# The first block's layer norms without barriers, and the inverse levels spread over four quarters of the array

## What is computed

```
x = layer_norm(x, ln0_g, ln0_b)
for l in range(DEPTH):                      # 2
    mix = hybrid_mixer(x, ...)              # pooling, differential attention, RWKV-7 in both directions
    x = layer_norm(alpha * x + mix, ln1_g[l], ln1_b[l])
    hid = square(relu(x @ w_up[l]))
    x = layer_norm(alpha * x + hid @ w_down[l], ln2_g[l], ln2_b[l])

def layer_norm(x, g, b):
    mu = mean(x); var = mean(square(x - mu))
    return (x - mu) * rsqrt(var + LN_EPS) * g + b
```

## Time and profile before

| | us |
|---|---|
| median of 3 runs | 4649.83 |
| lowest, highest | 4648.24, 4654.93 |
| the profiled execution | 4657.47 |
| its span, first to last instruction | 4655.7 |
| PE, DVE, ACT busy | 4436.1, 1408.8, 867.9 |
| mean granted TensorE clock | 0.968 |

### The profile page before, as it was taken

The page is one execution under the profiler, slowest core; times in us unless marked ns, Lnnn a source line. Parts: engine busy times, 40 slices in busy tenths (PEclk is TensorE's granted clock), DMA queues, the critical chain, the costliest instruction groups (busy, mean ns, idle before and its releaser), DMA issues.

```text
span 4655.7 us, 60696 instructions
## 1 busy us (share of the span) xinstructions
PE 4436.1 (95%) x25140; PEld 2927.2 (63%) x25140; DVE 1408.8 (30%) x3439; ACT 867.9 (19%) x2217; POOL 329.8 (7%) x274
## 2 busy tenths in 40 slices
PE   7899999989998999999998999899999999999999
PEld 3676674434443567775443444677887788788888
DVE  3665651020001556662111100331123331312232
ACT  3123320010000232221001000222222202222220
POOL 0122200000000022210000000000110000011000
PEclk8999999999999999999999999999999999999999
DMA  3001002212221110002221222111111121111111
GB/s 108 28 28 41 32 20 83 84 54 77 73 77 58 51 41 28 29 28 70 86 77 55 73 77 77 46 46 50 50 50 50 50 68 55 46 55 51 55 55 64
DMA packets 71343, 261.61 MB, mean 56 GB/s; under 512 B 7920, under 2 KB 7920, under 8 KB 70816
## 3 DMA queue, kind: packets, MB, share of 16 engines
q1 hardware_dynamic: 69168, 250.62, 15.7%
q10 hardware_dynamic: 1904, 7.11, 0.5%
HBM read 253.51 MB, written 4.19 MB: 55 GB/s over the span
## 4 chain that ended last, share of the span: by engine, by line
PE 91%; DVE 4%; ACT 3%; DVEq 1%; issue 1%; DMA 0%; ACTq 0%; SPq 0%
PE ps L2238 26%; PE ps L1420 25%; PE ps L2358 9%; PE ps L1589 4%; PE ps L2324 4%; PE ps L1439 2%; PE ps L1523 2%; PE ps L2268 2%; PE ps L824 2%; PE ps L831 1%; PE ps L790 1%; PE ps L2249 1%; PE ps L816 1%; PE ps L2259 1%; PE ps L1542 1%; PE ps L866 1%
## 5 line engine op out<-in xcount | busy, mean ns | idle before, releaser
L2238 PE MATMUL ps<-xT,ring 128*128 128x512 f32 x2656 | 1172.6, 600 | 58.0 <-ACTq L672 47.1
L2238 PEld LDWEIGHTS ps<-xT,ring 128*128 128x128 f32 x2656 | 507.3, 193 | 707.9 <-issue 707.9
L1420 PE MATMUL ps<-xT,ring 128*128 128x264 f32 (+2 forms) x3392 | 798.6, 391 | 17.3 <-DVE arena L1908 10.1
L1420 PEld LDWEIGHTS ps<-xT,ring 128*128 128x128 f32 (+1 forms) x3392 | 642.2, 193 | 137.4 <-DVE arena L1908 13.5
L2358 PE MATMUL ps<-arena,ring 128*128 128x512 f32 x1024 | 440.4, 592 | 2.4 <-ACT arena L2473 1.4
L2358 PEld LDWEIGHTS ps<-arena,ring 128*128 128x128 f32 x1024 | 194.2, 190 | 248.6 <-issue 248.6
L1420 PE MATMUL ps<-arena,ring 128*128 128x264 f32 (+1 forms) x1408 | 320.3, 385 | 2.3 <-DVEq L1809 2.3
L1420 PEld LDWEIGHTS ps<-arena,ring 128*128 128x128 f32 x1408 | 265.9, 191 | 46.4 <-issue 6.1
L1679 ACT ACTIVATE arena<-ps 128x264 f32<-128x264 f32 (+8 forms) x316 | 122.7, 389 | 710.4 <-PE ps L1420 618.2
L1053 ACT ACTIVATE arena<-ps 128x128 f32<-128x128 f32 (+1 forms) x268 | 103.2, 405 | 404.8 <-PE ps L2238 159.1
L2594 DVE TENSOR_TENSOR arena<-arena 128x512 f32<-128x512 f32 x64 | 44.3, 692 | 419.8 <-ACT arena L2473 419.8
(11 more groups left out here) (322 smaller groups left out, 5253.7 us busy)
## 6 DMA issues: line engine op xcount, KB each, us to landing
ring<-in_weights SPq DMA_DIRECT2D x467, 512.0 KB, 3.4
arena<-skew_dram ACTq DMA_DIRECT2D x8, 448.0 KB, 3.1
arena<-in_x SPq DMA_DIRECT2D x1, 2048.0 KB, 10.9
out_rows<-arena SPq DMA_DIRECT2D x8, 256.0 KB, 2.8
skew_dram<-arena ACTq DMA_DIRECT2D x4, 511.5 KB, 6.0
consts<-in_const SPq DMA_DIRECT2D x1, 1384.0 KB, 5.9
consts<-in_const ACTq DMA_DIRECT2D x1, 1252.0 KB, 5.5
arena<-in_buckets SPq DMA_DIRECT2D x1, 127.9 KB, 10.9
```

The lines of the kernel that those rows point to most:

```text
L1420: mm = pe.matmul(o[0:m, 0:cols.stop - cols.start], ws[:, k, 0:m], src[:, k, cols], start=k == 0, stop=k == nk - 1)
L2238: m = pe.matmul(o, w[:, k, :], src[:, k, 0:S], start=k == 0, stop=k == KD - 1)
```

## The change

Norms:
- The barriers go. PE waits for each tile of the normed `xT` by itself (`normed`), in the first projection behind a norm alone.
- Ahead of each norm but the first, DVE keeps a running sum `acc` of tiles 0 to 6 of `xT` as they are updated (`add_up`, one more tensor_tensor per tile from tile 1 to tile 6). The mean is then two matmuls: ones by `acc`, ones by tile 7. The first norm keeps 8.
- The mean isn't copied out: one scalar_tensor_tensor per tile subtracts it out of PSUM. The root reads the sum of squares from PSUM, with scale and bias. A one-element Sqrt ahead of the squares brings the table.
- Gain and bias: ACT does tiles 0 to 5, DVE tiles 6 and 7.
- In the first norm, the matmuls of the mean and of the squares come ahead of the bias lines on PE; ACT copies and stores the lines behind its part of the norm.

Inverse levels: for the second head the operands X, XT and W of block e lie in the other partition half, in the buffer of the other number where that is needed. `first_inverse`, `level_w` and `level_x` then use all four quarters in turn; `level_t` and both corners use the same ones as before. The number of instructions and their sizes stay.

```diff
-            def halves():
-
-                for n in range(NCH):
-                    for q in range(2):
-                        for h in range(2):
-                            e = q ^ h
-                            yield h, n, slice(HB * e, HB * e + HB), slice(HB * n, HB * n + HB)
+            half = [slice(HB * e, HB * e + HB) for e in range(2)]
+            quarters = [(n, h, e, slice(HB * n, HB * n + HB)) for n in range(NCH) for h in range(2) for e in (h, 1 - h)]
...
             def level_w(d, b, x):
...
-                for h, n, r, k in halves():
-                    m = pe.matmul(o[h][r, k], g1[d][h][r, n, 0, r], X[d][h][r, n, :], start=True, stop=True)
+                for n, h, e, k in quarters:
+                    r = half[e]
+                    m = pe.matmul(o[e][half[e ^ h], k], g1[d][h][r, n, 0, r], X[d][e ^ h][r, n, :], start=True, stop=True)
...
             def level_x(d, b):
...
-                for h, n, r, k in halves():
-                    m = pe.matmul(o[h][r, k], XT[d][h][r, n, :], W[d][h][r, n, :], start=True, stop=True)
+                for n, h, e, k in quarters:
+                    f = half[e ^ h]
+                    m = pe.matmul(o[e ^ h][half[e], k], XT[d][h][f, n, :], W[d][e][f, n, :], start=True, stop=True)
...
             def level_t(d, b):
...
-                for h, n, r, k in halves():
-                    m = pe.matmul(o[h][r, k], W[d][h][r, n, :], XT[d][h][r, n, :], start=True, stop=True)
+                for n in range(NCH):
+                    for e in range(2):
+                        for h in range(2):
+                            f = half[e ^ h]
+                            m = pe.matmul(o[h][f, HB * n:HB * n + HB], W[d][e][f, n, :], XT[d][h][f, n, :], start=True, stop=True)
...
+            def mean_of(it, bank):
+
+                pe.wait_ge(*at("ln_summed", it - 1))
+                pe.matmul(ps[:, bank, :], ones, acc, start=True, stop=False)
+                pe.wait_ge(*at("ln_ready", it, KD - 1))
+                pe.matmul(ps[:, bank, :], ones, xT[:, KD - 1, 0:S], start=False, stop=True).then_inc(STEPS["mean_made"][0], 1)
...
-                act.wait_ge(*at("ln_var", it))
-                act.activation(lnm[:, 1, :], lnm[:, 0, :], ACT.Sqrt).then_inc(STEPS["ln_root"][0], 1)
+                act.wait_ge(*at("var_made", it))
+                act.activation(lnm[:, 1, :], ps[:, banks[1], :], ACT.Sqrt, scale=1.0 / D, bias=lam[:, 8:9]).then_inc(STEPS["ln_root"][0], 1)
...
-                for j in range(KD):
+                for j in range(6):
                     act.wait_ge(*at("ln_scaled", it, j))
-                    act.activation(xT[:, j, 0:S], xT[:, j, 0:S], ACT.Identity, scale=g0[:, j:j + 1], bias=b0[:, j:j + 1])
-                act.drain()
+                    act.activation(xT[:, j, 0:S], xT[:, j, 0:S], ACT.Identity, scale=g0[:, j:j + 1], bias=b0[:, j:j + 1])\
+                       .then_inc(STEPS["ln_out_a"][0], 1)
```

More of the change, by code:

```diff
@@ L354, in build @@
         relu = rf.take(4, S)
+        acc = relu[:, 0, :]
         rl = Region()
@@ L2260, in turn, with mean_part, var_parts @@
                 tiles.close(m)
-            def layer_norm(base, it):
-                v = Maker(pe, lnV, base, v_made, v_taken)
-                for which, src, ready in (("mean", xT, "ln_ready"), ("var", sqr, "ln_sq")):
-                    o = v.open(which)
-                    for j in range(KD):
-                        pe.wait_ge(*at(ready, it, j))
-                        m = pe.matmul(o, ones, src[:, j, 0:S], start=j == 0, stop=j == KD - 1)
-                    v.close(m)
-                v.end()
+            def mean_part(it, bank, j):
+                pe.wait_ge(*at("ln_ready", it, j))
+                m = pe.matmul(ps[:, bank, :], ones, xT[:, j, 0:S], start=j == 0, stop=j == KD - 1, skip_group_check=True)
+                if j == KD - 1:
+                    m.then_inc(STEPS["mean_made"][0], 1)
+            def mean_of(it, bank):
[3 more added lines that the diff above has]
+                pe.matmul(ps[:, bank, :], ones, xT[:, KD - 1, 0:S], start=False, stop=True).then_inc(STEPS["mean_made"][0], 1)
+            def var_parts(it, bank):
+                for j in range(KD):
+                    pe.wait_ge(*at("ln_sq", it, j))
+                    m = pe.matmul(ps[:, bank, :], ones, sqr[:, j, :], start=j == 0, stop=j == KD - 1)
+                m.then_inc(STEPS["var_made"][0], 1)
             pe.wait_ge(c_loaded, 16)
@@ L2277, in _ @@
                 turn(a, f"x{j}", [xrow[:, t, j * P:(j + 1) * P] for t in range(4)])
+            for j in range(KD):
+                mean_part(0, BV[0], j)
+            var_parts(0, BV[1])
             pe.wait_ge(*at("relw", 0))
@@ L2383, in _, with layer_norm @@
                 act.drain().then_inc(STEPS["ln_ready"][0], 1)
-            for h in range(4):
-                for i in range(2):
-                    n = min(512, LINE - 512 * i)
-                    o = a.open(f"line{h}_{i}")
-                    a.close(act.activation(line[:, h, 512 * i:512 * i + n], o[:, 0:n], ACT.Copy))
-            a.end()
-            act.drain()
-            for h in range(4):
-                act.dma_start(skew_dram[h, :].rearrange("(p n) -> p n", n=LINE), line[:, h, 0:LINE])\
-                   .then_inc(skew_stored, 16)
-            act.wait_ge(skew_stored, 64)
-            def layer_norm(it, g0, b0, base, to_h=False):
+            def layer_norm(it, g0, b0, banks, to_h=False):
+                act.activation(lam[:, 9:10], ones[:, 0:1], ACT.Sqrt)
                 for j in range(KD):
@@ L2494, in _, with add_up @@
             dve.drain().then_inc(STEPS["relw"][0], 1)
-            def layer_norm(base, it):
-                v = Taker(dve, lnV, base, v_made, v_taken)
-                o = v.open("mean")
-                v.close(dve.tensor_scalar(lnm[:, 0, :], o, 1.0 / D, None, ALU.mult))
-                dve.drain()
+            dve.memset(lam[:, 8:9], LN_EPS)
+            dve.drain()
+            def add_up(j):
+                if 0 < j < KD - 1:
+                    dve.tensor_tensor(acc, xT[:, 0, 0:S] if j == 1 else acc, xT[:, j, 0:S], ALU.add)
+                    dve.drain()
+                if j == KD - 2:
+                    dve.sem_inc(STEPS["ln_summed"][0], 1)
@@ new lines, in layer_norm @@
+                for j in range(KD):
+                    dve.tensor_tensor(xT[:, j, 0:S], xT[:, j, 0:S], lnm[:, 0, :], ALU.mult).then_inc(STEPS["ln_scaled"][0], 1)
+                if to_h:
+                    return
+                dve.drain()
+                for j in range(6, KD):
+                    dve.tensor_scalar(xT[:, j, 0:S], xT[:, j, 0:S], g0[:, j:j + 1], b0[:, j:j + 1], ALU.mult, ALU.add)\
+                       .then_inc(STEPS["ln_out_v"][0], 1)
+                dve.drain()
+            l0 = K1_AT["ln0"][0]
```

136 lines of the change are left out of this document (61 added, 75 removed).

## The result

The changed kernel takes 4572.86 us (median; 4562.41 to 4580.16), the kernel before on the same chip 4652.38 (4648.24 to 4656.23). The ratio is 0.983, with a 95% interval from 0.981 to 0.985: 1.7% faster, 79.5 us. The forecast was 4574, and the time lies in its range.

What follows compares the result with a forecast made beforehand. PE, busy 95% of the span, was taken to bound the kernel, with 91% of the chain. Norms 50.5 plus levels 25 made 75.5 us: 4582 for a profiled execution, 4574 for the median; range 4560 to 4605.

Steps and rivals of the forecast that it cites:

- The norms: All five norms: shorter means, no copies of mean and variance, earlier projections; 50.5 us gained together.
- The running sum: Mean of a norm: two matmuls instead of eight, 5.34 us saved, with DVE's adds covered and costing nothing.
- The wait per tile: End of a norm: the projection needs only tile 0, starts 1.8 us after the scaling instead of 6.87, 5.1 earlier.
- The first norm: Bias lines moved behind the norm, made at half clock; first projection at 54.4 us, 5.4 gained (3.4 to 9.9).
- The norms behind the mixers: Layers 0 and 1: mean 5.34, copies 0.79 and 0.77, end 5.1; 12.0 us each, 24.0 for the two.
- The levels: Inverse levels and first inverses: four quarters at 14.6 ns a record; 3.1 us a group, 8 groups, 25 us gained.
- a quarter is a stream of its own: Inverse levels: each quarter takes about 58 ns a record, so four quarters in turn give 14.6 ns.
- rival 1: Inverse levels: four quarters go as two, 29.2 ns stays, the norms alone remain; 4599 us, chance 23%.
- rival 2: Inverse levels: a floor on record spacing leaves a third to half of the gain, 10 us; 4589 us, chance 16%.
- The five levels: Each group: a level takes 5.24 us instead of 5.74; four levels give 0.5 each, the fifth 0.2, 2.2 a group.
- The bounds that the prediction gave for the levels: Gain in the levels: 0 if four quarters go no faster, 60 us at 1.5 a level; 35 without the wait for W.
- Rival 3: Inverse levels: the clock falls, a level takes 8.0 us; 4691 us, chance 4%. Against: PE never stands longer than 0.7 us.

Runs made afterwards that it cites:

- eight_sums: The changed kernel with the mean of four norms made of eight matmuls again, no running sum and no adds on DVE: 4598.05 us, ratio 0.988.
- wait_all: The changed kernel, but the first projection behind a norm waits for all eight tiles before its first matmul: 4589.82 us, ratio 0.985.
- after_again: The changed kernel itself, the same program in another execution: 4571.74 us, ratio 0.982 of the kernel before.
- norms_only: The changed kernel with the old order of quarters in the inverse levels: 4607.15 us, ratio 0.989 of the kernel before.
- w_twice: The changed kernel with each matmul of level_w issued twice, 64 records more per level: 4627.95 us, ratio 0.994 of the kernel before.
- levels_only: The kernel before with the new inverse levels alone: 4633.6 us, ratio 0.9955.
- rows_apart: The changed kernel with the 16 matmuls of W, X and first inverse sorted, one row half's eight before the other's: 4584.54 us, ratio 0.984.

## Why the forecast came out

**The norms** (50.5, measured 54.0 by stages and 50.5 as a difference of medians). Each step is seen. The running sum is worth 4.8 to 5.2 us a norm, forecast 5.34 (`eight_sums`), and its adds are covered. The wait per tile gives 4.5 to 4.8 of the 5.1 forecast for the end of a norm (`wait_all`). The first norm came out at 5.4, since the lines did run at half clock, which was the choice there. The norms behind the mixers gave 1.1 and 1.5 more than 12.0: the sum of squares takes 7.15 us instead of 8.69. The stretch had a mean clock of 0.81 before, in the window's row of the kernel before:

```profile
1003.00:1011.90 8.90, 8.68 (x16) 3.60 (x16) 3.58 (x7) 5.52 (x9) 0.00 (x0) 0.81 0.01 2
```

I had kept the 8.69 as if it were work.

**The levels** (25, measured 18.7). That a quarter is a stream of its own was right, and with it that 32 records take 0.46 us; rival 1 and rival 2 fall by it. The two first inverses gave 0.91 us a group, forecast 0.94, thus 7.3 of the 18.7. The five levels gave 11.4 in all, forecast 17.6, and here a step failed: the one that counted matmuls by their spacing alone. At 15 ns a record PE asks for more instructions than come, and 11.3 us of stops that weren't in the sum are on the path. The prediction's argument that PE never stands longer than 0.7 us in a level fell with it: a stop of 1.17 us is shown above.

Without the stops the term would have been up to 30, so something else was mis-sized, in the other direction. It isn't the bare level: one with neither a stop nor other work of PE in it lasts 5.25 us (the fourth in layer 0's first group) or 5.45 (the third in layer 1's first), forecast 5.24. The trace puts 31 us down to DVE in the eight groups and not 60, but these can't be set side by side: the trace counts PE as busy until a matmul's end, 0.22 us behind its start, while the forecast counted waits from the spacing of starts. With the stops taken out, which is an estimate, since DVE catches up while PE stands, the first three levels gave 0.4 to 0.6 us each, forecast 0.5. The fourth gave about 1.0 in the six groups in which PE has other work in it; its waits for DVE are 0.05 to 0.22 us there. The fifth gave 0.6, forecast 0.2. The forecast priced the fourth as if it were bare and the fifth too low; why the fifth gave more isn't shown.

The bounds that the prediction gave for the levels don't follow from its own numbers: 5.74 less 3.74 is 2.0 us a level, 80 in all and not 60, and 25 with the wait for W of 0.7 a level taken out is 53 and not 35. The measured term lies below all of them.

**What was not in the sum**: 22.4 us of the profiled pair. 16.1 of it lies behind the last corner of each layer, where the kernel before runs at half clock for 17 us. The windows there, 9 to 26 us behind the corner of layer 0, of the kernel before and of the changed one:

```profile
648.00:665.00 17.00, 16.40 (x70) 14.59 (x72) 6.56 (x20) 3.95 (x12) 0.00 (x0) 0.50 0.00 0
```

```profile
625.00:642.00 17.00, 16.36 (x134) 14.57 (x134) 11.48 (x36) 6.94 (x21) 0.00 (x0) 1.00 0.01 2
```

134 records in the time of 70. It isn't a sure gain. In `after_again` the half clock stays away in layer 0 and is back for 17 us in layer 1:

```profile
2031.00:2050.00 19.00, 18.51 (x80) 15.40 (x81) 7.16 (x22) 4.17 (x13) 0.00 (x0) 0.55 0.00 1
```

In the traces of the kernel before and of `norms_only` it is there for 17 us in four layers of four. With the new levels, 20 layers of 10 traces (`w_twice` aside), it is missing in eight, shorter in ten (7 to 14 us) and full in two; `w_twice` has it for 17 and 14 us. What the new levels do to PE ahead of it, standing now and then and starting matmuls more densely, changes how the clock falls; by which rule, these runs don't settle. The clock as a whole also goes with the spread of the changed kernel: over four of its executions the span goes from 4560.6 to 4578.4 us as the mean clock goes from 0.975 to 0.972, and their product stays within 4 us. Over the whole trace the kernel before spends 296 us at half clock, the changed one 228 and `after_again` 252.

So that the forecast's time was met within 2 us is in part luck. Its terms were off in opposite ways: the levels gave 6.3 less, the norms 3.5 more, and the clock outside the edited stages gave some us that weren't in the sum, more in the profiled execution and fewer in the median one. How many of the median's 79.5 us are the clock's isn't shown; the two halves, run alone, sum to 74.5, and the difference lies within the intervals.

**Rival 3**, the clock falling inside the levels, didn't come in the changed kernel: the granted clock is 1.00 through the levels of all eight groups, and in the window from 155 to 184 us PE is busy 84%. In `levels_only` it falls 1.1 us before one corner, and in `w_twice` 4.7 us in the levels are at half clock.

## What to carry to other kernels

When matmuls are small, count instructions as well as their spacing: once they follow each other at 15 ns, the supply of instructions is a limit of its own, and it shows as "issue" idle time at equal distances in records, beside packets of 16 KB. In a norm across engines, the whole-tensor barriers are cheap to find and to remove: a wait per tile and a running sum kept beside the matmuls gave some 10 of the 13 us behind a mixer. And read the clock in the stretches behind the edit too, on more than one execution, before a gain or a loss there is put down to the edit.

## What the runs showed that I had not expected

- All four 64x64 quarters in turn: 32 records in 0.46 us, starts down to 7 ns apart inside a set of four quarters, 15.4 ns in the median batch. One quarter is a stream of about 58 ns a record in every kernel here.
- Two quarters of the same rows alternate as well as two of different rows, two records per 58 ns in both. And PE takes up records of a free quarter ahead of the busy ones: in `rows_apart` four start together in the middle of a batch.
- PE stops of 0.1 to 1.7 us with no semaphore, 126 or 127 float32 records apart, at the same record in two executions, with a packet of 16 KB 1.0 to 1.6 us behind most of them; 39.1 us of them with 256 records in a level, 11.3 with 192, 0.1 with the same 192 at 29 ns.
- A DVE operand in PSUM costs nothing against SBUF in the subtraction: 0.70 us for 128x512 in both.
- Ln and exp on ACT need a table load of 1.28 us between them, 0.64 us for the exp of 128x512.
